# Seven groups of dense expert tiles in two parts of the activation buffer, the next group's U between a group's U and V, four gathered rows moved forward

## The chip, the cores and the metric

The kernel runs on one core of one Trainium2 chip. The metric is the time of one execution on the device, in microseconds (us), the median of several. Everything is float32.

## The reference, cut to what matters

One layer over 512 tokens of width 2048: a mixing part (attention and a recurrence), attention into 256 memory tokens, and an expert part with 16384 experts of one neuron each, eight heads, 16 experts a head and token. The change touches the expert part alone.

```python
def peer_ffn(x, w_pq, sub_keys1, sub_keys2, peer_u, peer_v):
    q = (xt @ w_pq).reshape(T, PEER_HEADS, PEER_QUERY)
    s1, s2 = first half of q . sub_keys1, second half of q . sub_keys2
    v1, i1 = lax.top_k(s1, PEER_TOPK)
    v2, i2 = lax.top_k(s2, PEER_TOPK)
    ...
    top_s, pos = lax.top_k(cand_s, PEER_TOPK)
    idx = jnp.take_along_axis(cand_i, pos, axis=-1)
    gate = jax.nn.softmax(top_s, axis=-1)
    ...
    u_sel = jnp.take(peer_u, ib, axis=0)
    act = jax.nn.gelu(jnp.einsum('thkd,td->thk', u_sel, xb), approximate=False) * gb
    v_sel = jnp.take(peer_v, ib, axis=0)
    return jnp.einsum('thk,thkd->td', act, v_sel)
x = layer_norm(DN_ALPHA * x + y_ffn, ln3_g[l], ln3_b[l])
```

(The line of s1, s2 is shortened; `xb`, `ib`, `gb` are a block's tokens, expert numbers and gates.)

## The kernel before

**Two ways for two halves of the tokens.** The 512 tokens are four blocks of 128. For blocks 0 and 1 the kernel gathers the chosen experts: 128 choices a token and block, so 256 *rows*. A row r is one load of `peer_u` and one of `peer_v` (128 partitions x 8 KB, 1 MB each, an indirect DMA on GpSimd's queue, lines 611 and 622), a dot product on VectorE (line 1739), a Gelu of four rows at a time on ScalarE (`gelu_rows`, line 1318) and an addition into the block's sum on VectorE (line 1750). The dot of row r+4 stands just ahead of the addition of row r. U loads have two buffers, V loads two; a third of each comes in early in the stream. For blocks 2 and 3 (256 tokens) TensorE multiplies with all 16384 experts, in 128 *tiles* of 128: a U tile is 16 matmuls 128x256 (line 1050), ScalarE puts the Gelu of two tiles into the buffer G (`gelu_dense`, line 1333), VectorE multiplies eight tiles at a time with their gates (`weigh(q)`, line 1800), and V quads (4 tiles by 512 output columns, 8 matmuls 128x512, line 1077) sum them in PSUM. In the trace a matmul counts as two records.

**Groups, positions, chunks.** The tiles are cut into groups g of 40, 32, 32 and 24 (`TILES`). G holds one group. TensorE's order is U0, V0, U1, V1, U2, V2, U3, V3, where Ug are a group's U tiles and Vg its V quads: for each of four column chunks c, TILES[g]/4 quads. Each U tile and each V quad takes 1 MB of weights (line 458, SyncE's queue, a ring of four slots). From V0 on they are numbered: a *position* is one U tile or one V quad, 216 in all. V0 is 0 to 39, U1 40 to 71, V1 72 to 103, U2 104 to 135, V2 136 to 167, U3 168 to 191, V3 192 to 215.

**What TensorE waits for in the stream.** A V quad of chunk 0 waits for the product of its eight tiles (`g_ready`). The first quad of a chunk waits until the sum of the chunk two earlier has left its banks (`x_added`, `add_dense`, line 1809 in V0, line 1811 later). A U tile waits for the Gelu of the tiles eight earlier (`gl_done`). Each of these stands in an engine's own list behind other work.

**What stands in VectorE's and ScalarE's lists.** Rows are spread over the positions by `half_pos`: rows 2k and 2k+1 are *due* at a position, and VectorE's program runs through the positions in order, with the products (at `weigh_pos`), the rows due, two last expert choices (at 2 and 3 by number, positions 8 and 15) and, after a chunk's last position, its sum. It doesn't wait for TensorE to reach a position; it can run behind it. `HALVES_BEFORE` (34) says that 68 rows stand ahead of V0. ScalarE's list has the same positions. The rows ahead of V0 are placed by hand (`some_rows(n)`, and `d_route(n, between)`, which puts `between` rows between the two halves of an expert choice). GpSimd issues the row loads in order and, among them, the gates of eight tiles (`load_gates`, from tile 40 on), at places that `GATES_AFTER` works out.

```python
def half_pos(k):
    return 3 + (k - HALVES_BEFORE) * (POSITIONS - 6) // (2 * RSTEPS - HALVES_BEFORE)
...
                if c == 0 and l % 2 == 0:
                    pe.wait_ge(g_ready, FIRST[g] // 8 + l // 2 + 1)
...
                    elif l == 0:
                        pe.wait_ge(x_added, 2 * (g * 4 + c - 2) + tb + 1)
```

**The end.** Block 0's norm (`norm`, line 1488 and on) stands after U3, block 1's within V3 ahead of the last chunk's sum, blocks 2 and 3 are normed after it and written out.

## Time and profile before

| | us |
|---|---|
| median of 3 runs | 3290.2 |
| range of the runs | 3282.97 to 3298.95 |
| the profiled execution | 3295.16 |
| its span, first to last instruction | 3293.5 |
| mean granted TensorE clock over the span | 0.982 |
| TensorE busy with matmuls | 3119.8 (95%) |
| VectorE busy | 2073.9 (63%) |
| moved by DMA | 1029.69 MB, mean 313 GB/s |

Times in the rows count from the span's start. A row of a timeline gives start, duration, engine, line, operation, what it writes and reads, how many were merged (x) and in square brackets the idle time ahead of it and what ended it. Matmul ends are modelled: a merged stretch of 640 records that takes 276 us is TensorE going at one pace. A wait on several semaphores is put down to the one that came last.

### The profile page before, as it was taken

To read this page: it belongs to the slowest core of one execution; us is meant where nothing else is said; L and a number is where in the kernel's file an instruction comes from. 1 tells how busy PE (TensorE), PEld (TensorE's weight loads), DVE (VectorE), ACT (ScalarE), POOL (GpSimd) and SP (SyncE) were. 2 spreads that over 40 slices of the span, in tenths; PEclk is the share of its full clock that TensorE was granted. 3 is DMA by queue.
4 is the path that set the end of the run, shared out by engine and by line. 5 is a ranking of instruction groups with operands and counts; after the bars stand their busy time and mean duration, and the time that the engine had idled before them with its cause. 6 is when DMAs were issued, how large, how long until landed. Compare 5 with 4: busy or idle time off the path is not lost.

```text
span 3293.5 us, 27033 instructions
## 1 busy us (share of the span) xinstructions
PE 3119.8 (95%) x10342; PEld 1889.4 (57%) x10342; DVE 2073.9 (63%) x2874; ACT 367.9 (11%) x653; POOL 682.0 (21%) x557
## 2 busy tenths in 40 slices
PE   8999998899999898999989999999999999999797
PEld 5444443334445577678874447884458853478443
DVE  5356532342668779889997766656566666656675
ACT  1233212320101211112210000000000000000000
POOL 0000000000021134322222333222222333223240
PEclk9999999999999999999999999999999999999899
DMA  6222221047797678998998999999999999999985
GB/s 267 77 77 70 86 65 44 10 166 261 294 408 309 258 316 358 417 387 305 350 350 350 389 422 421 421 415 417 421 421 421 419 419 416 422 421 421 412 368 233
DMA packets 152515, 1029.69 MB, mean 313 GB/s; under 512 B 16464, under 2 KB 21712, under 8 KB 35664
## 3 DMA queue, kind: packets, MB, share of 16 engines
q0 software_dynamic: 78512, 557.88, 41.6%
q1 hardware_dynamic: 73888, 470.24, 36.4%
q8 instruction: 76, 1.25, 0.2%
q14 instruction: 39, 0.32, 0.0%
HBM read 1007.08 MB, written 20.97 MB: 312 GB/s over the span
## 4 chain that ended last, share of the span: by engine, by line
DMA 41%; PE 33%; DVE 18%; issue 4%; ACT 2%; POOL 2%; DVEq 0%; SPq 0%; ACTq 0%; POOLq 0%
DMA arena<-peer_v,arena 40%; PE ps L693 10%; DVE arena L1750 7%; PE ps L1077 4%; PE ps L845 3%; DVE arena L1788 2%; DVE arena L1739 2%; PE ps L935 2%; PE ps L863 2%; PE ps L770 1%; PE ps L1050 1%; PE ps L799 1%; ACT arena L1117 1%; POOL arena L611 1%; PE ps L785 1%
## 5 line engine op out<-in xcount | busy, mean ns | idle before, releaser
L1077 PE MATMUL ps<-arena 128*128 128x512 f32 x2048 | 884.8, 595 | 52.8 <-DVE arena L1800 52.0
L1050 PE MATMUL ps<-arena 128*128 128x256 f32 x4096 | 898.3, 381 | 9.6 <-ACT arena L1333 8.9
L1050 PEld LDWEIGHTS ps<-arena 128*128 128x128 f32 x4096 | 778.7, 191 | 118.9 <-ACT arena L1333 9.7
L1750 DVE SCALAR_TENSOR_TENSOR arena<-arena 128x2048 f32<-128x2048 f32 x256 | 601.8, 2351 | 298.8 <-DMA arena<-peer_v,arena 233.1
L1739 DVE CUSTOM_DVE_ANT_0 arena<-arena 128x2048 f32<-128x2048 f32 x256 | 586.2, 2290 | 288.4 <-DMA arena<-peer_u,arena 286.8
L1077 PEld LDWEIGHTS ps<-arena 128*128 128x128 f32 x2048 | 390.6, 191 | 544.8 <-issue 490.6
L611 POOL DMA_INDIRECT arena<-peer_u,arena x256 | 346.8, 1354 | 1108.3 <-DVE arena L1739 909.3
L622 POOL DMA_INDIRECT arena<-peer_v,arena x256 | 309.2, 1208 | 755.0 <-DVE arena L1750 725.8
L693 PE MATMUL ps<-arena 128*128 128x512 f32 x800 | 345.2, 592 | 1.1 <-ACT arena L1117 1.1
L693 PEld LDWEIGHTS ps<-arena 128*128 128x128 f32 x800 | 151.9, 190 | 192.2 <-issue 192.2
L1117 ACT ACTIVATE arena<-ps 128x512 f32<-128x512 f32 (+3 forms) x247 | 145.2, 611 | 774.9 <-PE ps L855 138.8
L845 PE MATMUL ps<-arena 128*128 128x512 f32 x512 | 220.8, 592 | 0.9 <-ACT arena L1117 0.9
L1318 ACT ACTIVATE arena<-arena 128x4 f32<-128x4 f32 x64 | 13.1, 205 | 1545.1 <-DVE arena L1739 1545.0
L845 PEld LDWEIGHTS ps<-arena 128*128 128x128 f32 x512 | 97.0, 190 | 122.3 <-issue 120.5
L863 PE MATMUL ps<-arena 128*128 128x512 f32 x320 | 139.3, 593 | 2.5 <-ACT arena L1117 2.5
L935 PE MATMUL ps<-arena 128*128 128x256 f32 x640 | 139.2, 379 | 1.7 <-ACT arena L1117 1.7
L935 PEld LDWEIGHTS ps<-arena 128*128 128x128 f32 x640 | 121.3, 190 | 18.9 <-ACT arena L1117 2.2
L863 PEld LDWEIGHTS ps<-arena 128*128 128x128 f32 x320 | 60.6, 190 | 76.2 <-issue 72.5
L1788 DVE TENSOR_TENSOR arena<-arena 128x1024 f32<-128x1024 f32 x64 | 78.1, 1220 | 11.4 <-ACT arena L1117 10.5
L1062 PE MATMUL ps<-arena 128*128 128x128 f32 x512 | 70.0, 281 | 13.3 <-DVE arena L1790 13.2
L1062 PEld LDWEIGHTS ps<-arena 128*128 128x128 f32 x512 | 64.4, 191 | 20.4 <-DVE arena L1790 18.8
L1557 DVE TENSOR_TENSOR arena<-arena 128x512 f32<-128x512 f32 x16 | 11.0, 688 | 99.9 <-ACT arena L1169 99.9
(179 smaller groups left out, 1804.9 us busy)
## 6 DMA issues: line engine op xcount, KB each, us to landing
arena<-peer_ut SPq DMA_DIRECT2D x128, 1024.0 KB
arena<-peer_vt SPq DMA_DIRECT2D x128, 1024.0 KB
arena<-w_row SPq DMA_DIRECT2D x52, 1024.0 KB
arena<-w_mix SPq DMA_DIRECT2D x48, 1024.0 KB
arena<-w_once SPq DMA_DIRECT2D x74, 512.0 KB, 3.5
arena<-w_feat SPq DMA_DIRECT2D x20, 1024.0 KB
dense_gates<-arena SPq DMA_DIRECT2D x8, 2048.0 KB, 7.3
arena<-dense_gates POOLq DMA_DIRECT2D x11, 1024.0 KB, 24.2
```

The lines of the kernel that those rows point to most:

```text
L611: pool.indirect_dma_start(UB[e], None, peer_u, bass.IndirectOffsetOnAxis(ap=IDX[:, r:r + 1], axis=0)).then_inc(u_full[e], 16)
L622: pool.indirect_dma_start(VB[e], None, peer_v, bass.IndirectOffsetOnAxis(ap=IDX[:, r:r + 1], axis=0)).then_inc(v_full[e], 16)
L693: last = pe.matmul(out_ap, tile(t + half)[:, k * P:(k + 1) * P], A[:, kt * S:(kt + 1) * S], start=(kt == 0), stop=(kt == KT - 1))
L845: last = pe.matmul(bank(k), Y[:, b * D + kt * P:b * D + (kt + 1) * P], w[:, i * 512:(i + 1) * 512], start=(kt == NL), stop=(kt == NL - 1))
L863: last = pe.matmul(bank(k), XT[:, kt * P:(kt + 1) * P], w[:, i * 512:(i + 1) * 512], start=(kt == 0), stop=(kt == KT - 1))
L935: last = pe.matmul(ps[:, k + f // 2, (f % 2) * DT:(f % 2 + 1) * DT], w[:, kt * P:(kt + 1) * P], XTD[:, kt * DT:(kt + 1) * DT], start=(kt = ...
L1050: last = pe.matmul(ps[:, (e // 2) % 4, (e % 2) * DT:(e % 2 + 1) * DT], w[:, kt * P:(kt + 1) * P], XTD[:, kt * DT:(kt + 1) * DT], start=(kt ...
L1077: last = pe.matmul(bank(4 + (c % 2) * 2 + tb), G[:, t * DT + tb * P:t * DT + (tb + 1) * P], w[:, i * 512:(i + 1) * 512], start=(t == 0), s ...
L1117: return act.activation(dst, src, ACT.Copy)
L1739: dve.tensor_tensor_reduce(UB[e], UB[e], xrow(b), 1.0, 0.0, ALU.mult, ALU.add, DOT[r // 4 % 2][:, r % 4:r % 4 + 1]).then_inc(u_free, 1)
L1750: dve.scalar_tensor_tensor(out=acc, in0=VB[e], scalar=AV[r // 4 % 2][:, r % 4:r % 4 + 1], in1=acc, op0=ALU.mult, op1=ALU.add).then_inc(v_f ...
L1788: link(dve.tensor_tensor(oh, IOTA.unsqueeze(1).unsqueeze(1).broadcast_to([P, 2, 4, NK]), turn[:, 0:2, here].unsqueeze(3).broadcast_to([P, ...
```

## The change

The tiles are cut into seven groups of 24, 16, 24, 16, 24, 16 and 8. G is 40 tiles long as before, in two parts: groups 0, 2, 4, 6 at slots 0 to 23, groups 1, 3, 5 at slots 24 to 39 (`slot_of`). The head (`HEAD`, 40 tiles) is the U of groups 0 and 1; then the order is V0, U2, V1, U3, V2, U4, V3, U5, V4, U6, V5, V6. Positions: V0 0 to 23, U2 24 to 47, V1 48 to 63, U3 64 to 79, V2 80 to 103, U4 104 to 127, V3 128 to 143, U5 144 to 159, V4 160 to 183, U6 184 to 191, V5 192 to 207, V6 208 to 215. The product of eight tiles stands 13, 21 or 29 positions after the start of its U group; those of the head at positions 0, 1, 2, 10 and 20. `HALVES_BEFORE` is 36: four more rows ahead of V0, two between the sums of d.wo and two in `d_route(4)`, with their Gelu moved ahead of `d_pq(0)` on ScalarE. The other rows are due up to position 202 (before 210). Block 0's norm and block 1's now stand after the last row, in V6; the gain and bias that they need take the gates' two buffers and are loaded on GpSimd's queue, not SyncE's.

```diff
-TILES = [40, 32, 32, 24]
-FIRST = [sum(TILES[:g]) for g in range(4)]
-GCAP = max(TILES)
+TILES = [24, 16, 24, 16, 24, 16, 8]
+NG = len(TILES)
+FIRST = [sum(TILES[:g]) for g in range(NG)]
+HEAD = TILES[0] + TILES[1]
+GCAP = HEAD
+STREAM = [(kind, g) for k in range(NG) for kind, g in (("V", k), ("U", k + 2)) if g < NG]
...
+def slot_of(e):
+
+    g = group_of(e)
+    return e - FIRST[g] + TILES[0] * (g % 2)
...
-HALVES_BEFORE = 34
+HALVES_BEFORE = 36
...
-    return 3 + (k - HALVES_BEFORE) * (POSITIONS - 6) // (2 * RSTEPS - HALVES_BEFORE)
+    return 3 + (k - HALVES_BEFORE) * (POSITIONS - 14) // (2 * RSTEPS - HALVES_BEFORE)
...
-    if q < TILES[0] // 8:
-        return (0, 1, 2, 3, 5)[q]
...
+    if q < HEAD // 8:
+        return (0, 1, 2, 10, 20)[q]
+    g = group_of(8 * q)
+    start = sum(TILES[h] for _, h in STREAM[:STREAM.index(("U", g))])
+    return start + 8 * q - FIRST[g] + 13
...
+            def load_gain3(k):
+                pool.wait_ge(g_ready, NK // 8 - 1 + k)
+                pool.dma_start((GAIN3_G, GAIN3_B)[k], gains[6 + k:7 + k, :].partition_broadcast(P)).then_inc(gain3_in, 16)
...
-                if p == TILES[0] + 6:
+                if p == HEAD + 14:
                     load_gates(4)
...
             exps("b1.max", PR, 6, 0, "b1.exp")
+            gelu_rows()
             d_pq(0)
...
                 if c == 1:
-                    some_rows(2)
+                    some_rows(4)
...
-            d_route(4, 2)
+            d_route(4, 4)
...
+                if g == NG - 1:
+                    rows_until(POSITIONS)
+                    dve.wait_ge(gain3_in, 32)
+                    dve.wait_ge(v_free, HK)
+                    norm(ACC, ACC, GAIN3_G, GAIN3_B, dve_tick).then_inc(y_ready, 1)
                 for c in QUAD:
...
-                    if g == 3 and c == 3:
-                        rows_until(POSITIONS)
+                    if g == NG - 1 and c == 2:
                         dve.wait_ge(v_free, 2 * HK)
                         norm(ACC1, ACC1, GAIN3_G, GAIN3_B, dve_tick).then_inc(y_ready, 1)
                     add_dense(g, c)
```

TensorE, from the last head tiles on: first before, then changed. Lines 1050 and 1074 are the U matmuls (16 a tile), 1077 and 1102 those of V (8 a quad).

```order
L1050 MATMUL ps<-arena 128x256 x88
L1077 MATMUL ps<-arena 128x512 x320
L1050 MATMUL ps<-arena 128x256 x512
L1077 MATMUL ps<-arena 128x512 x256
L1050 MATMUL ps<-arena 128x256 x512
L1077 MATMUL ps<-arena 128x512 x256
L1050 MATMUL ps<-arena 128x256 x384
L1077 MATMUL ps<-arena 128x512 x192
```

```order
L1074 MATMUL ps<-arena 128x256 x88
L1102 MATMUL ps<-arena 128x512 x192
L1074 MATMUL ps<-arena 128x256 x384
L1102 MATMUL ps<-arena 128x512 x128
L1074 MATMUL ps<-arena 128x256 x256
L1102 MATMUL ps<-arena 128x512 x192
L1074 MATMUL ps<-arena 128x256 x384
L1102 MATMUL ps<-arena 128x512 x128
L1074 MATMUL ps<-arena 128x256 x256
L1102 MATMUL ps<-arena 128x512 x192
L1074 MATMUL ps<-arena 128x256 x128
L1102 MATMUL ps<-arena 128x512 x192
```

A group's V now follows the U of the group after it; the last 192 are V5 (128) and V6 (64).

VectorE, at the sums of d.wo (lines 1649 and 1671) ahead of blocks 2 and 3's second norm: first before, then changed. Lines 1739 and 1761 are dots, 1750 and 1772 additions of a row.

```order
L1649 SCALAR_TENSOR_TENSOR arena<-arena,ps 128x512 x2
L1762 TENSOR_TENSOR arena<-arena 128x4
L1739 ISA arena<-arena 128x2048
L1739 ISA arena 128x1
L1750 SCALAR_TENSOR_TENSOR arena<-arena 128x2048
L1739 ISA arena<-arena 128x2048
L1739 ISA arena 128x1
L1750 SCALAR_TENSOR_TENSOR arena<-arena 128x2048
L1649 SCALAR_TENSOR_TENSOR arena<-arena,ps 128x512 x4
L1488 BN_STATS arena<-arena 128x6 x4
```

```order
L1772 SCALAR_TENSOR_TENSOR arena<-arena 128x2048
L1761 ISA arena<-arena 128x2048
L1761 ISA arena 128x1
L1772 SCALAR_TENSOR_TENSOR arena<-arena 128x2048
L1761 ISA arena<-arena 128x2048
L1761 ISA arena 128x1
L1772 SCALAR_TENSOR_TENSOR arena<-arena 128x2048
L1671 SCALAR_TENSOR_TENSOR arena<-arena,ps 128x512 x4
L1510 BN_STATS arena<-arena 128x6 x4
```

Two more rows (the last of the four are shown) stand ahead of the last four sums of d.wo and the norm that follows them.

## Rows read from the trace of the kernel before

**Rows 1.** The page's 40 slices of the span: granted clock, then DMA rate.
```profile
PEclk9999999999999999999999999999999999999899
GB/s 267 77 77 70 86 65 44 10 166 261 294 408 309 258 316 358 417 387 305 350 350 350 389 422 421 421 415 417 421 421 421 419 419 416 422 421 421 412 368 233
```

**Rows 2.** TensorE's timeline from V0's start on (columns as said above).
```profile
1725.39 276.35 PE L1077 MATMUL ps<-arena 128*128 128x512 f32 x640 [9.52 <-DVE arena L1800]
...
2388.39 55.17 PE L1077 MATMUL ps<-arena 128*128 128x512 f32 x128 [0.84 <-DVE arena L1811]
...
2557.77 112.42 PE L1050 MATMUL ps<-arena 128*128 128x256 f32 x512 [3.70 <-ACT arena L1333]
2670.02 41.36 PE L1077 MATMUL ps<-arena 128*128 128x512 f32 x96
2725.32 180.31 PE L1077 MATMUL ps<-arena 128*128 128x512 f32 x416 [13.93 <-DVE arena L1800]
...
2979.90 99.16 PE L1050 MATMUL ps<-arena 128*128 128x256 f32 x448 [5.21 <-ACT arena L1333]
3078.89 27.63 PE L1077 MATMUL ps<-arena 128*128 128x512 f32 x64
3135.04 139.04 PE L1077 MATMUL ps<-arena 128*128 128x512 f32 x320 [28.52 <-DVE arena L1800]
```

**Rows 3.** Stretches: busy us (x) by engine, PEclk, DMA share, GB/s; last, line 1750 alone.
```profile
2711.40:2725.30 13.90, 0.00 (x0) 0.00 (x0) 9.25 (x7) 0.69 (x2) 5.18 (x5) 0.62 1.01 420
3106.50:3135.00 28.50, 0.02 (x1) 0.00 (x0) 23.66 (x32) 0.00 (x0) 7.91 (x5) 0.57 0.86 352
1725.00:1900.00 175.00, 174.61 (x404) 77.40 (x405) 125.93 (x201) 6.41 (x10) 54.16 (x36) 0.99 0.92 367
...
1900.00:2711.00 811.00, 235.17 (x100) 1.00 1.01 420
```

**Rows 4.** VectorE's timeline: the product of tiles 24 to 31.
```profile
1742.06 2.29 DVE L1800 TENSOR_TENSOR arena<-arena 128x2048 f32<-128x2048 f32 x1 [8.93 <-DMA arena<-dense_gates]
```

**Rows 5.** VectorE's timeline: sums after positions 39 and 87, the product of position 136.
```profile
2025.25 1.28 DVE L1809 SCALAR_TENSOR_TENSOR arena<-arena,ps 128x512 f32<-128x512 f32 x2
...
2387.56 1.28 DVE L1811 TENSOR_TENSOR arena<-arena,ps 128x512 f32<-128x512 f32 x2
...
2722.97 2.28 DVE L1800 TENSOR_TENSOR arena<-arena 128x2048 f32<-128x2048 f32 x1
```

**Rows 6.** VectorE's timeline: the two norms (the last row ends at the second) and the end.
```profile
3122.26 2.47 DVE L1488 BATCH_NORM_STATS2 arena<-arena 128x6 f32<-128x512 f32 x4
...
3245.47 2.47 DVE L1488 BATCH_NORM_STATS2 arena<-arena 128x6 f32<-128x512 f32 x4
...
3253.65 2.35 DVE L1494 SCALAR_TENSOR_TENSOR arena<-arena 128x2048 f32<-128x2048 f32 x1
3274.12 1.29 DVE L1811 TENSOR_TENSOR arena<-arena,ps 128x512 f32<-128x512 f32 x2 [18.12 <-PE ps L1077]
```

**Rows 7.** Ahead of V0, VectorE's and TensorE's timelines, in order of time.
```profile
1105.79 2.28 DVE L1739 CUSTOM_DVE_ANT_0 arena<-arena 128x2048 f32<-128x2048 f32 x1
...
1114.74 2.47 DVE L1649 SCALAR_TENSOR_TENSOR arena<-arena,ps 128x512 f32<-128x512 f32 x4
...
1138.15 1.97 PE L855 MATMUL ps<-arena 128*128 128x128 f32 x16 [2.06 <-DVE arena L1494]
...
1174.20 0.16 DVE L1762 TENSOR_TENSOR arena<-arena 128x4 f32<-128x4 f32 x1 [17.38 <-ACT arena L1318]
...
1257.78 3.40 PE L985 MATMUL ps<-arena 128*128 128x128 f32 x16 [5.84 <-ACT arena L1117]
```

**Rows 8.** VectorE's timeline: additions of two rows in a run of four.
```profile
954.00 2.35 DVE L1750 SCALAR_TENSOR_TENSOR arena<-arena 128x2048 f32<-128x2048 f32 x1 [1.80 <-issue]
...
962.03 2.35 DVE L1750 SCALAR_TENSOR_TENSOR arena<-arena 128x2048 f32<-128x2048 f32 x1 [2.37 <-DMA arena<-peer_v,arena]
```

**Rows 9.** The page's DMA issues: out<-in, queue, kind, count, KB each.
```profile
arena<-peer_vt SPq DMA_DIRECT2D x128, 1024.0 KB
```

More of the change, by code:

```diff
@@ L84, with group_of @@
 SLOTS = 4
-TILES = [40, 32, 32, 24]
-FIRST = [sum(TILES[:g]) for g in range(4)]
-GCAP = max(TILES)
+TILES = [24, 16, 24, 16, 24, 16, 8]
[4 more added lines that the diff above has]
+STREAM = [(kind, g) for k in range(NG) for kind, g in (("V", k), ("U", k + 2)) if g < NG]
+def group_of(e):
+    return max(g for g in range(NG) if FIRST[g] <= e)
+def slot_of(e):
+    g = group_of(e)
+    return e - FIRST[g] + TILES[0] * (g % 2)
 PQ_AFTER = [2, 5, 8, 11]
@@ L631, in _ @@
                     v_row(4 * j + s)
-                    for q in range(5, NK // 8):
+                    for q in range(5, NK // 8 + 2):
                         if GATES_AFTER[q] == 4 * j + s:
-                            load_gates(q)
+                            if q < NK // 8:
+                                load_gates(q)
+                            else:
+                                load_gain3(q - NK // 8)
         @block.tensor
@@ L1076, in v_quad @@
                         t = 4 * l + i
-                        last = pe.matmul(bank(4 + (c % 2) * 2 + tb), G[:, t * DT + tb * P:t * DT + (tb + 1) * P],
+                        at_g = slot_of(FIRST[g] + t) * DT + tb * P
+                        last = pe.matmul(bank(4 + (c % 2) * 2 + tb), G[:, at_g:at_g + P],
                                          w[:, i * 512:(i + 1) * 512], start=(t == 0), stop=(t == TILES[g] - 1))
                 used(last, f"V{g}.{c}.{l}")
-            for t in range(TILES[0]):
+            for t in range(HEAD):
                 if ONEHOT_FROM <= t < ONEHOT_FROM + DT // 16:
@@ L1101, in _ @@
                     last.then_inc(tb_mm, 1)
-            for g in range(4):
-                for c in QUAD:
-                    for l in range(TILES[g] // ET):
-                        v_quad(g, c, l)
-                if g < 3:
-                    for t in range(TILES[g + 1]):
-                        u_tile(g + 1, t)
+            for kind, g in STREAM:
+                if kind == "U":
+                    for t in range(TILES[g]):
+                        u_tile(FIRST[g] + t)
+                else:
+                    for c in QUAD:
+                        for l in range(TILES[g] // ET):
+                            v_quad(g, c, l)
             assert order == PE_STEPS and at[0] == W_AT[W_UNITS[-1]]
@@ L1439, in _ @@
             gelu_rows()
-            for t in range(t, TILES[0], 2):
-                gelu_dense(0, t)
-                if t == TILES[0] - 6:
+            for t in range(t, HEAD, 2):
+                gelu_dense(t)
+                if t == HEAD - 6:
                     gate_exps(12)
@@ L1454, in _ @@
             p = 0
-            for g in range(4):
-                for _ in range(TILES[g]):
+            for kind, g in STREAM:
+                for t in range(TILES[g]):
+                    if kind == "U" and t % 2:
+                        gelu_dense(FIRST[g] + t - 1)
                     rows_until(p)
                     p += 1
-                if g < 3:
-                    for t in range(TILES[g + 1]):
-                        if t % 2:
-                            gelu_dense(g + 1, t - 1)
-                        rows_until(p)
-                        p += 1
             rows_until(POSITIONS)
@@ L1942, in _ @@
                     add_dense(g, c)
-                    if g == 3:
+                    if g == NG - 1:
                         last = last_stats(c)
-                if g < 3:
-                    for t in range(TILES[g + 1]):
-                        for i in range(TILES[g + 1] // 8):
-                            if weigh_pos(FIRST[g + 1] // 8 + i) == p:
-                                weigh(FIRST[g + 1] // 8 + i, i)
-                        rows_until(p)
-                        p += 1
-                    if g == 2:
-                        dve.wait_ge(gain3_in, 32)
-                        dve.wait_ge(v_free, HK)
-                        norm(ACC, ACC, GAIN3_G, GAIN3_B, dve_tick).then_inc(y_ready, 1)
-                if g == 3:
-                    link(last)
+            link(last)
             for tb in range(DB):
```

112 lines of the change are left out of this document (57 added, 55 removed).

## The prediction

> **What bounds the kernel now.** I read the slices of the page first, then TensorE's timeline from 1725 us with what ended each of its waits, and last, in the same stretch, VectorE's timeline and what DMA moved. In the slices the clock row is nearly all nines, and from 1894 to 3128 us the core moves 412 to 422 GB/s [rows 1]: two resources are full at once, TensorE and DMA. In the stream that the change rearranges, TensorE runs 40 positions in 276.35 us, 6.91 us each, and stands still five times: 0.84, 3.70, 13.93, 5.21 and 28.52 us, 52.2 us in all [rows 2]. The two long ones are waits for the gates' product (line 1800), 52.0 us with the 9.52 ahead of V0; the 3.70 and 5.21 are Gelus (line 1333), the 0.84 a sum (line 1811) [rows 2]. 216 positions at 6.91 us are 1492 us; V0's start to the last matmul's end is 3274.1 - 1725.4 = 1548.7 us [rows 2]. So 52.2 us are stalls and 4.6 us slower matmuls around them (the granted clock is 0.62 and 0.57 over the two long stalls, between the levels of 1.2 and 2.4 GHz [rows 3]). Those 56.8 us are all that any order of this stream could win on TensorE.
>
> Why is the product late? V2 starts at 2670.0 and V3 at 3078.9 [rows 2], but the products due then (positions 136 and 192) run at 2723.0 and 3132.7 (the end of the second stall) [rows 2, 5]: **VectorE is 53 us, nearly eight positions, behind its own list.** It does not wait for TensorE; it waits for row loads. From 1900 to 2711 us it adds 100 rows [rows 3] while six gate loads go through the same queue: 206 loads in 811 us, 3.94 us each, at 420 GB/s in total [rows 3]. A row is two loads, 7.87 us.
>
> **The lag, as a sum.** Before, 2 rows are due every 2.234 positions, 0.895 a position: VectorE needs 0.895 x 7.87 = 7.04 us for a position that TensorE does in 6.91, so the lag grows 0.14 us a position and 3.9 us with each gate load. Test: the rows due by position 38 end at 2025.3, with TensorE at 38 at 1725.4 + 38 x 6.91 = 1988, a lag of 37; the sum of chunk 1 of V1 (rows due by 87) comes at 2387.56 against 2326, a lag of 61 [rows 2, 5]. The rule gives 37 + 49 x 0.14 + 4 x 3.9 = 60. It holds.
>
> **Part 1: the products leave the path: -56.8 us.** In the new order eight tiles' product is placed 13 positions or more after the start of their U group, and their V group begins 27 positions or more after that (11 for V6). At a lag of 60 us the margin of 27 x 6.91 = 187 us isn't touched. The 42.4 us of long stalls go; the 9.8 us of short ones and the 4.6 us of slow clock I take off here too and count again in part 3.
>
> The matmuls, 10342 of them, the products and the sums of the rest are as before in number, but for 24 more sums (56 for 32) of 0.64 us each on VectorE [rows 5], which has idle time beside every row, and TensorE takes a U or a V position in the same 6.91 us (16 of U, the slow clock after a stall among them, take 112.42 [rows 2]): the new order itself costs nothing.
>
> **Part 2: four rows earlier: +11 us ahead of V0.** Two of them stand between the sums of d.wo. There VectorE is on the path: its sums for d.wo 2 and 3 start at 1114.74, as soon as two rows are done, the norms follow, and TensorE waits 2.06 us for the second one at 1138.15 [rows 7]. Two rows cost at least 2 x 4.47 us (1105.79 to 1114.74 for two, dot and add [rows 7]) and up to 8 us each where both buffers are empty (954.00 to 962.03 [rows 8]): 9 to 16, here about 10, since the first two find their data there. After b1's probabilities VectorE sits 17.38 us until the Gelu at 1174 [rows 7]; the change puts that Gelu earlier, four rows fit in the gap, and it takes up the first delay. But in d_route(4) four rows stand where two stood, with buffers just drained: 9 to 16 us again, and this chain is what TensorE waits for at 1257.78 (5.84 us) [rows 7]. So both engines come 8 to 15 us late to tile U0, and no wait for anything else hides it. I take 11, near the lower end, since the data of at least two rows is there.
>
> **Part 3: what is late next: +44 us.** A V group's chunk c writes into the banks of chunk c-2, so TensorE waits at chunk 2 for the sum of chunk 0, and that sum stands in VectorE's list behind all rows due by then. With 40 and 32 tiles a chunk is 10 or 8 positions and VectorE may be 9 positions (62 us) late; at a lag of 61 the stall was 0.84 us [rows 2]. With 16 tiles a chunk is 4 positions: the last rows ahead of the sum are due 5 positions before it is needed in V1 and 6 in V3 and V5, less 2 us for the sum: 33 and 39 us. With 24 tiles it is 7 or 8, 46 and 53 us. The lag is above that.
> The new lag: two rows are due every 202/92 = 2.196 positions, 0.911 a position; 0.911 x 7.87 - 6.91 = 0.26 us of growth a position. The product of tiles 24 to 31 no longer stands ahead of the first rows; it waited 8.93 us for its gates and took 2.28 [rows 4], so the rows start 11 us sooner. At position 38 the lag is 37 - 11 + 35 x 0.126 = 30. From there to 202, where the last rows are due, it would grow by 164 x 0.26 = 43 us and by 10 loads of gates and gain, 39 us: 112 us if TensorE never stood. It can't: V5 lets it pass with 39 at most, some 37 at position 202. The 75 us between are taken off by stalls. In a stall all of DMA goes to the rows: 420 GB/s in the 13.9 us stall [rows 3], against 2 x 1.0486 MB in 7.87 us, 267 GB/s. So a microsecond of stall takes off 1.57, and the stalls come to 75 / 1.57 = **48 us**, most of it at chunk 2 of V3 (about 20), the rest in V1, V4, V5 and U4.
> The other bound is bytes. Before, the last row ends at 3245.4, 1520 us after V0's start [rows 6]. Now 8 row loads are gone and, with TensorE at position 207, some 4.5 weight loads aren't due yet: 12.5 loads of 1024 KB [rows 9] at 421 GB/s [rows 1], 2.49 us each, 31 us. VectorE's first norm, 10.5 us long, starts at 3122.26 between two rows, in a stall whose stretch moved only 352 GB/s [rows 3, 6]; it now comes after the last row: 10 us. The earlier start puts 11 us of rows, 2.9 MB, into a stretch that averaged only 367 GB/s [rows 3]: 6 us. The last row would end 1473 us after V0's start, which at position 202 (1395 us) and a lag of 37 leaves **41 us** of stalls. I take 44, between the two, and 4 us of slow clock (before 4.6 for 52.2).
>
> The page "DMA: Bandwidth & Descriptors" of the Trainium skill (Where 436 GB/s comes from) says that for HBM to SBUF the HBM side, about 358 GB/s, binds. The trace disagrees: 420 GB/s and more over most of 1200 us [rows 1, 3]. By the page's figure a load would cost 2.93 us, the 12.5 loads 37 us and the second bound 35 us of stalls; the trace decides.
>
> **The end** stays: the last group of 8 tiles needs the last row's end + 13 us (a norm of 10.5, 3245.47 to 3256.00 [rows 6], and a sum) by position 212; at 207.5 + 2 positions there are 17 us to spare. The second norm has the two positions of chunk 2, 13.8 us for 10.5. The gain's second half is now the last load of GpSimd's queue, behind the last row; it lands about one load, 4 us, later, within the 17. From the last matmul's end to the end of the span 19.4 us stay [rows 6].
>
> **Sum.** -56.8 + 11 + 44 + 4 = +2 us: 3295.2 us of the profiled execution become 3297; it lies 5 us above the median of the three runs, 3290.2, which becomes **3292**.
>
> **Rivals.** *A, faster: the narrow groups don't hold TensorE.* If only V6 binds (last row + 13 us at position 212) the stalls are 1473 + 13 - 1464 = 22 us and the sum is -56.8 + 11 + 22 + 2 = -22: 3268. With the delay of part 2 absorbed as well, 3258. For it: the lag thresholds rest on one stall of 0.84 us. Against: list and banks are plain in the code, and the 3.70 and 5.21 us stalls show that a lag of 60 us bites elsewhere too. *B, slower: a stall doesn't speed the rows.* If rows alone don't use the freed DMA time, the stalls are 75 us at factor 1: +31 us, 3323; it turns to slower by 0.5% from a factor under about 1.3 (59 us of stalls). For it: over the long stall only 352 GB/s moved. Against: that stretch holds the norm; the other one moved 420 [rows 3]. [...] *C, the head costs more:* 16 us twice with no gap to take it up, +32 - 11: 3313, slower. *D, the change doesn't do what it says:* products still late. It would take a lag of 187 us; under 1%.
>
> **How the numbers follow.** Forecast (stalls 38 to 52, head 8 to 15): 56%, 3283 to 3304. A 22%, B 10%, C 9%, the rest no case named here. 16.5 us (0.5%) is about what a measurement can tell from no change. The forecast's range lies within it. Faster 0.24, same 0.56, slower 0.20. The range reaches to A's and C's times: 3266 to 3314.
>
> **What would show it.** In the trace after: no wait of V's matmul for the product except ahead of V0; V0 starting near 1736; waits of the V line on the sum's line, largest in V3 and V5, 30 to 45 us in all; DMA at 420 in them; the last row about 1473 us after V0's start. Wrong if the waits for sums are under 25 us or over 60, or V0 starts before 1730 or after 1745.

## The result, and the profile after

Of the kernel before, 7 runs have a median of 3288.98 us, of the changed kernel, 7 runs, 3308.26 us (3300.25 to 3320.02). The ratio is 1.0058, with a 95% interval of 1.004 to 1.0076: **slower by 0.6%**, where I had forecast 3292 and no change; 3308 lies within the range. The profiled execution of after is the fastest of its seven (3300.25 us, span 3298.6), that of before lies 6 us above the median of its seven: the two profiles are 5 us apart where the medians are 19.

TensorE's timeline of after from V0's start on (start, length, engine, line, operation, count, in brackets the idle time ahead and what ended it). Line 1102 is V's matmul, 1074 U's, 1823 the product, 1834 the sum of the groups after V0, 1772 the addition of a row:

```profile
1735.24 106.13 PE L1102 MATMUL ps<-arena 128*128 128x512 f32 x240 [9.38 <-DVE arena L1823]
1845.24 64.55 PE L1102 MATMUL ps<-arena 128*128 128x512 f32 x144 [3.87 <-DMA arena<-peer_vt]
1909.63 165.92 PE L1074 MATMUL ps<-arena 128*128 128x256 f32 x768
2075.39 82.68 PE L1102 MATMUL ps<-arena 128*128 128x512 f32 x192
2166.17 30.16 PE L1102 MATMUL ps<-arena 128*128 128x512 f32 x64 [8.10 <-DVE arena L1834]
...
2637.24 55.10 PE L1102 MATMUL ps<-arena 128*128 128x512 f32 x128
2708.99 57.58 PE L1102 MATMUL ps<-arena 128*128 128x512 f32 x128 [16.66 <-DVE arena L1834]
...
2965.66 84.72 PE L1102 MATMUL ps<-arena 128*128 128x512 f32 x192 [6.18 <-DVE arena L1834]
...
3167.46 111.98 PE L1102 MATMUL ps<-arena 128*128 128x512 f32 x256 [6.89 <-DVE arena L1834]
```

Against [rows 2] the two waits for the product, 13.93 and 28.52 us, are gone and so are the Gelus'; in their place stand four waits for a sum, 37.8 us, and one of 3.87 for a V load. Five stalls are 41.7 us, where five were 52.2. From V0's start to the start of the last matmul it was 1548.1 us, now it is 1543.6 (to that matmul's end, as the prediction counts, 1548.7 and 1544.2).

The view of stretches, over three of the sum waits, and line 1772 alone over the stretch of [rows 3] (busy us by engine, then granted clock, DMA share, GB/s), then VectorE's timeline at the longest wait:

```profile
2158.00:2166.20 8.20, 0.10 (x2) 0.06 (x1) 5.42 (x5) 0.00 (x0) 3.04 (x4) 0.68 1.01 423
2692.30:2709.00 16.70, 0.04 (x2) 0.04 (x1) 12.48 (x10) 0.00 (x0) 6.72 (x4) 0.63 1.01 408
...
3160.50:3167.50 7.00, 0.11 (x2) 0.07 (x1) 5.44 (x5) 0.20 (x1) 0.94 (x1) 0.78 1.02 424
...
1900.00:2711.00 811.00, 236.00 (x101) 0.98 1.01 419
```

```profile
2700.97 2.35 DVE L1772 SCALAR_TENSOR_TENSOR arena<-arena 128x2048 f32<-128x2048 f32 x1 [2.77 <-issue]
...
2705.90 2.35 DVE L1772 SCALAR_TENSOR_TENSOR arena<-arena 128x2048 f32<-128x2048 f32 x1 [0.23 <-DMA arena<-peer_v,arena]
2708.17 1.28 DVE L1834 TENSOR_TENSOR arena<-arena,ps 128x512 f32<-128x512 f32 x2
```

TensorE stands, its clock is granted at 0.63 to 0.78 of the full one, DMA still moves 408 to 424 GB/s, and VectorE takes rows as they land; the sum that TensorE needs comes right behind the last row listed ahead of it.

Ahead of V0, in order of time, to compare with [rows 7] (VectorE's rows, d.wo's sums, then TensorE's waits):

```profile
1103.87 2.35 DVE L1772 SCALAR_TENSOR_TENSOR arena<-arena 128x2048 f32<-128x2048 f32 x1 [1.40 <-DMA arena<-peer_v,arena]
...
1112.31 2.35 DVE L1772 SCALAR_TENSOR_TENSOR arena<-arena 128x2048 f32<-128x2048 f32 x1 [2.10 <-DMA arena<-peer_v,arena]
1114.58 2.48 DVE L1671 SCALAR_TENSOR_TENSOR arena<-arena,ps 128x512 f32<-128x512 f32 x4
...
1127.55 3.68 PE L880 MATMUL ps<-arena 128*128 128x128 f32 x16 [8.76 <-DVE arena L1516]
1137.99 3.68 PE L880 MATMUL ps<-arena 128*128 128x128 f32 x16 [6.76 <-DVE arena L1516]
...
1268.42 3.79 PE L1010 MATMUL ps<-arena 128*128 128x128 f32 x16 [13.96 <-ACT arena L1143]
```

TensorE now waits 15.5 us for the two norms (before 2.06) and 13.96 for the dense keys (before 5.84). In the profile of after everything stands 12 us earlier by then: its first row is added at 910.67 us, in before at 922.52. So V0's start, 1735 against 1725, hides part of what the head lost.

**A ruler.** From the first row's addition to V0's start it is 802.9 us in before, and 802.1, 802.3, 802.3 and 809.6 in the four runs below that leave the four rows where they were; with the four rows moved it is 824.6 in after and 827.7 to 834.9 in six others. The means are 803.8 and 830.5. The runs' tables below give, in us: *stream*, V0's start to the start of the last matmul; *stalls*, TensorE's idle time in it; *last row*, from V0's start to the end of the last addition of a row; *tail*, the start of the last matmul to the end of the span. Each from the profile of one execution; ratios are to the kernel before, with 95% intervals.

| kernel | ratio | stream | stalls | last row | tail |
|---|---|---|---|---|---|
| before | | 1548.1 | 52.2 | 1520 | 20.0 |
| after | 1.0058 [1.004, 1.0076] | 1543.6 | 41.7 | 1474 | 19.8 |

### The profile page after: what moved, and what is told of

It is laid out like the page before. It is cut to its first block, busy times and chain, and to the rows that moved or that the text cites. A ratio compares the mean times of both kernels' runs of the same rounds, so it can differ in the third digit from the quotient of the medians.

```text
span 3298.6 us, 27067 instructions
## 1 busy us (share of the span) xinstructions
PE 3117.6 (95%) x10342; PEld 1888.6 (57%) x10342; DVE 2089.0 (63%) x2898; ACT 370.1 (11%) x653; POOL 682.7 (21%) x559
## 3 DMA queue, kind: packets, MB, share of 16 engines
q0 software_dynamic: 78800, 559.97, 41.7%
## 4 chain that ended last, share of the span: by engine, by line
DMA 40%; PE 33%; DVE 19%; issue 4%; POOL 2%; ACT 2%; DVEq 0%; ACTq 0%; SPq 0%; POOLq 0%
DMA arena<-peer_v,arena 40%; PE ps L718 10%; DVE arena L1772 7%; PE ps L1102 5%; PE ps L870 3%; DVE arena L1810 2%; DVE arena L1761 2%; PE ps L960 2%; PE ps L888 2%; PE ps L795 1%; PE ps L1074 1%; ACT arena L1143 1%; DVE arena L1699 1%; PE ps L810 1%; POOL arena L633 1%
## 5 line engine op out<-in xcount | busy, mean ns | idle before, releaser
L1102 PE MATMUL ps<-arena 128*128 128x512 f32 x2048 | 895.5, 600 | 51.1 <-DVE arena L1834 37.8
L633 POOL DMA_INDIRECT arena<-peer_u,arena x256 | 336.9, 1316 | 1084.5 <-DVE arena L1761 882.8
L644 POOL DMA_INDIRECT arena<-peer_v,arena x256 | 318.6, 1244 | 755.2 <-DVE arena L1772 736.6
L960 PEld LDWEIGHTS ps<-arena 128*128 128x128 f32 x640 | 123.2, 193 | 19.7 <-ACT arena L1143 2.2
L1086 PE MATMUL ps<-arena 128*128 128x128 f32 x512 | 70.0, 281 | 13.2 <-DVE arena L1812 13.1
L1086 PEld LDWEIGHTS ps<-arena 128*128 128x128 f32 x512 | 64.4, 191 | 20.4 <-DVE arena L1812 18.7
```

Of the source, the lines that this page charges most:

```text
L633: pool.indirect_dma_start(UB[e], None, peer_u, bass.IndirectOffsetOnAxis(ap=IDX[:, r:r + 1], axis=0)).then_inc(u_full[e], 16)
L644: pool.indirect_dma_start(VB[e], None, peer_v, bass.IndirectOffsetOnAxis(ap=IDX[:, r:r + 1], axis=0)).then_inc(v_full[e], 16)
L960: last = pe.matmul(ps[:, k + f // 2, (f % 2) * DT:(f % 2 + 1) * DT], w[:, kt * P:(kt + 1) * P], XTD[:, kt * DT:(kt + 1) * DT], start=(kt = ...
L1102: last = pe.matmul(bank(4 + (c % 2) * 2 + tb), G[:, at_g:at_g + P], w[:, i * 512:(i + 1) * 512], start=(t == 0), stop=(t == TILES[g] - 1))
```

## Experiments

**My theory:** the new order gains little in the stream, four rows ahead of V0 cost what they give back, and the sums wait since rows that the transfers bring late are listed ahead of them. Rivals: another cause of the sums' waits; a cheap head; a loss in the order alone.

### The order alone, the rows alone, and after once more

The rows alone are the kernel before with these lines changed; the order alone is the changed kernel with the same lines changed back:

```diff
-HALVES_BEFORE = 34
+HALVES_BEFORE = 36
+            gelu_rows()
-                    some_rows(2)
+                    some_rows(4)
-            d_route(4, 2)
+            d_route(4, 4)
```

> The change without its four moved rows: the new order of groups, 68 rows ahead of V0, 188 rows due by position 202. Theory (the end is set by how fast DMA brings rows and weights, and the stalls in V are where VectorE's lag is taken off): V0 starts near 1725 us as before the change (1735 with the rows moved), eight row loads more lie in the stream, 2.49 us each, so the waits for sums grow from 38 us to 55 to 62 us and the last row ends some 1496 us after V0's start (1476 changed). The run is about 10 us slower than the changed kernel, ratio to before 1.007 to 1.011. Rival (the ten microseconds at the head are what made the change slow, and the order costs nothing): 10 us faster than the changed kernel, ratio to before 1.000 to 1.003.

> The kernel before with the four rows moved ahead of V0 and nothing else. Theory: V0 starts 10 us later; the stream has eight loads less and its lag grows 0.15 us a position less, so the five stalls shrink from 52 us to about 32; ratio to before 0.995 to 0.999. Rival (rows at the head cost their 10 us and give nothing back, since VectorE's lag is not what delays the products): ratio 1.002 to 1.004.

> The changed kernel once more, for a second profile beside the others of this series. The profile at hand is its fastest run (3300 us; the median of seven is 3308). Expected: ratio 1.004 to 1.008, four waits for sums, 38 to 48 us in all, and the difference between a 3300 and a 3310 run in the stalls of the stream, not ahead of V0.

| kernel | ratio | stream | stalls | last row | tail |
|---|---|---|---|---|---|
| order alone | 1.0055 [1.0041, 1.007] | 1569.7 | 67.1 | 1494 | 19.7 |
| rows alone | 1.0008 [0.9993, 1.0023] | 1526.5 | 30.4 | 1499 | 20.0 |
| after again | 1.0062 [1.0048, 1.0075] | 1544.2 | 44.4 | 1472 | 19.7 |

**The loss comes without the four rows.** The rest of the change alone costs 0.55%, and its stream is 21.6 us longer than before. This kernel holds more than the new groups, though: its rows are due by position 202 instead of 210, and the norms and a gates' load have moved too. No run takes these apart, but the paced kernel without the four rows, below, has the same groups with the rows due later, and is no slower than before. So the groups by themselves need not lose; most likely they do together with rows listed this early. TensorE's timeline of the order alone:

```profile
2719.67 56.62 PE L1102 MATMUL ps<-arena 128*128 128x512 f32 x128 [29.58 <-DVE arena L1833]
...
3177.69 112.94 PE L1102 MATMUL ps<-arena 128*128 128x512 f32 x256 [15.90 <-DVE arena L1833]
```

The wait at V3's chunk 2 is as long as the longest product wait that the order removes. The four rows shorten the stream by 21.6 us in the old order and by 26.1 in the new one (1569.7 to 1543.6), yet the ratio moves by +0.0008 and +0.0003: so the head costs 24 us (21.6 + 0.0008 x 3290) and 27 (26.1 + 1), to within some 5 and 8 us by the ratios' intervals; the ruler says 26.7. My expectations had each wrong by this one number: I gave the rows alone 0.995 to 0.999 (measured 1.0008) and the order alone 1.007 to 1.011 (measured 1.0055), though the stalls came as told, 30.4 us for 32 and 58.5 us of sum waits for 55 to 62. TensorE's waits for the norms and the dense keys in the head of the rows-alone kernel (1090 to 1300 us; engine, line, for whom, us, times, longest) are 36.1 us, against 12.1 in the same stretch of before:

```profile
PE ps L855 <- DVE arena L1495: 17.4, 2, 10.7
PE ps L985 <- ACT arena L1117: 13.7, 2, 12.6
PE ps L985 <- DVE arena L1650: 5.0, 1, 5.0
```

After once more repeats the stream within 1 us. I had expected the spread between runs to be in the stream; between these two profiled executions it is ahead of V0 (1735.2 and 1744.2).

### Which pair costs the head

Each takes the kernel before and moves two of the four rows. The edit below is that of the pair at d.wo; the other has `d_route(4, 4)` in place of `some_rows(4)`. Both also put the Gelu ahead of `d_pq(0)`, as the change does, and since 35 halves need one Gelu of rows fewer ahead of V0 than 36, ScalarE's last one before the stream is left out.

```diff
-HALVES_BEFORE = 34
+HALVES_BEFORE = 35
...
+            gelu_rows()
             d_pq(0)
...
-            gelu_rows()
             for t in range(t, TILES[0], 2):
...
-                    some_rows(2)
+                    some_rows(4)
```

> The kernel before with one pair of rows moved alone: two more rows behind the second d.wo addition, so 35 halves instead of 34 stand ahead of the stream. Theory (the moved rows find their buffers empty: 7 to 9 us a row instead of 4.6, and TensorE then waits for the norms of the dense streams): the waits for those norms grow from 2 us to 12 to 16 us, the activation products start 10 to 14 us later than in the kernel before (1720 to 1725 us there), the stream from there to the last product is 10 to 12 us shorter than 1548; ratio 0.999 to 1.002. Rival (the head's loss comes from the fourth routing, not from here): norm waits stay below 6 us, the products start within 5 us of before, ratio 0.996 to 0.998.

> The kernel before with the other pair alone: four rows instead of two in the fourth routing. Theory: the norm waits stay at 2 us, the wait of the dense key transposes grows from 5.8 us to 11 to 14 us, the products start 7 to 10 us later than before, the stream is 10 to 12 us shorter; ratio 0.998 to 1.001. Rival (this pair is free, it lies beside other work): products start within 3 us of before, ratio 0.996 to 0.998.

| kernel | ratio | stream | stalls | first row to V0 |
|---|---|---|---|---|
| pair at d.wo | 1.0078 [1.0053, 1.0103] | 1540.0 | 44.1 | 845.7 |
| pair at the route | 1.0069 [1.0043, 1.0094] | 1539.8 | 43.6 | 838.9 |

The pair at d.wo, then the pair at the route, TensorE's waits from 1090 to 1300 us:

```profile
PE ps L855 <- DVE arena L1494: 17.1, 2, 10.3
PE ps L985 <- ACT arena L1117: 8.7, 3, 6.4
```

```profile
PE ps L889 <- ACT arena L1117: 14.9, 1, 14.9
PE ps L985 <- ACT arena L1117: 7.4, 4, 3.8
PE ps L855 <- DVE arena L1494: 2.0, 1, 2.0
```

The pair at d.wo makes TensorE wait 15 us more for the norms (17.1 for 2.1), a little over the 12 to 16 us expected. Under the other pair it is not the rows that TensorE waits for. ScalarE's timeline of that kernel shows what stands ahead of the wait at line 889:

```profile
1179.39 0.21 ACT L1318 ACTIVATE arena<-arena 128x4 f32<-128x4 f32 x1 [14.83 <-DVE arena L1739]
1179.50 1.01 ACT L1117 ACTIVATE arena<-ps 128x1024 f32<-128x1024 f32 x1
```

The eviction that TensorE needs (line 1117) stands behind a Gelu of rows (line 1318) that waits 14.83 us for its dots: with the Gelu ahead of `d_pq(0)`, every later one stands one place earlier in ScalarE's list, and here the rows that it takes are not yet done. In before, with fewer rows ahead, TensorE waits 1.3 us at this line. So the 14.9 us come with the second edit. The same holds for what comes after. U0's start to V0's start is 449 us in both kernels and 426 to 432 in every other one here; from 1290 to 1760 us ScalarE's Gelus of rows wait 131.3 us for dots in both, in nine waits, and 24.1 us, in one, in before and in the rows-alone kernel. I had expected ratios of 0.999 to 1.002 and 0.998 to 1.001; the measured 1.0078 and 1.0069 carry this edit and say nothing of the pairs.

The stretch ahead of it does: from the first row's addition to U0's start it is 370 to 378 us in the five kernels without the move (mean 374), 396.5 with the pair at d.wo, and 397 to 407 in the seven with all four rows (mean 402). **The pair at d.wo costs about 22 of the 28 us**, the pair at the route some 6, to within about 5 us, since each kernel has one profile. A kernel with the Gelu moved and no rows was not run.

### Sums earlier in VectorE's list

```diff
             def position(p):
+                if p in sums:
+                    add_dense(*sums[p])
...
-                    add_dense(g, c)
+                    if g in (0, NG - 1):
+                        add_dense(g, c)
```

(`sums` holds the sums of V1 to V5, each four positions earlier than its own.)

> The changed kernel with the sums of V1 to V5 four positions earlier in VectorE's list, so that they no longer stand behind rows due in the last four positions. Theory: TensorE's 38 us of waits for these sums go, but the rows' loads still need their bytes: the last row ends 5 to 15 us later than 1476 us after V0's start, and the last group's chunk 2 waits for it. Gain against the changed kernel 12 to 22 us, ratio to before 0.999 to 1.003. Rival 1 (only the place of the sums made the change slow): the whole 38 us and some 8 us of slow clock behind the stalls go, ratio 0.992 or less. Rival 2 (the waits move to Gelus, products or weights within the stream): no gain, ratio 1.005 or more.

Measured: ratio 1.0049 [1.0032, 1.0066]; stream 1536.9, stalls 37.3. TensorE's waits in the stream:

```profile
PE ps L1075 <- ACT arena L1359: 20.4, 2, 13.5
PE ps L1103 <- DVE arena L1835: 13.2, 1, 13.2
```

The sums' waits fall from 37.8 to 13.2 us, and 20.4 us of waits for Gelus appear: ScalarE has the dense Gelus behind those of rows, and they wait for the same late rows. Only 7 us of the stream are gained, and the ratio can't be told from the changed kernel's (1.0062 beside it); I had expected 0.999 to 1.003. It came nearer the second rival, that the waits move. With a lag as large as this one, moving one kind of work ahead of the rows brings up the next.

### Is it the transfers?

Two kernels take bytes from V's weight loads and leave every list as it is. In both, half of each V tile's weights isn't loaded, so they compute something else.

```diff
+                if unit[0] == "V":
+                    sp.dma_start(W2[s][0:64, :], src[0:64, :]).then_inc(wb_full[s], 16)
```

> The changed kernel with the weight loads of the V tiles cut to the upper 64 of 128 partitions: every V load carries half its bytes, and half of each V tile's weights is left as it was, so the output is another. Nothing else in any list moves. Theory (rows are late since the transfers move 417 to 422 GB/s and no more, so a sum listed behind rows waits for bytes): with about 54 MB fewer between the first product and the last row the rows keep up with their places, the sum waits fall from 38 us to under 8 us, products' start to last product 1500 to 1512 us; the rate drops below 400 GB/s. Rival (the sums wait for VectorE's own work or for how the row loads are issued): sum waits stay above 25 us, the stream above 1530 us.

```diff
+                if unit[0] == "V":
+                    sp.dma_start(W2[s][:, 0:PW // 2], src[:, 0:PW // 2]).then_inc(wb_full[s], 16)
```

> The changed kernel with the V weight loads cut to half their columns on all 128 partitions: packets of 4096 bytes (181 ns each in the changed kernel's trace) in place of 8192 bytes (314 ns), so each of the V loads gives the 16 DMA engines about 1.1 us back; half of each V tile's weights is left as it was, so the output is another. (With the upper 64 partitions alone the packets of 8192 bytes took 413 to 512 ns instead of 314 and the rows came later, not earlier.) Theory (sums wait since the rows ahead of them in VectorE's list are late by what the transfers can carry): with 110 us of transfer time less, the rows keep up with their places, sum waits fall from 38 us to under 8 us, products' start to last product 1500 to 1515 us. Rival (the sums wait for VectorE's own work or for how row loads are issued): sum waits stay above 25 us and the stream above 1530 us.

| kernel | ratio | stream | stalls | last row | tail |
|---|---|---|---|---|---|
| upper 64 partitions | one run, 3393.3 us | 1617.2 | 111.3 | 1557 | 19.7 |
| half the columns | 0.9908 [0.9879, 0.9936] | 1491.4 | 1.7 | 1397 | 19.7 |

The same stretch, within V1, of the one and of the other:

```profile
2100.00:2150.00 50.00, 49.45 (x116) 21.59 (x114) 27.09 (x19) 1.38 (x4) 15.02 (x12) 1.00 1.01 301
```

```profile
2100.00:2150.00 50.00, 50.00 (x118) 22.23 (x117) 38.65 (x29) 0.41 (x2) 18.04 (x17) 1.00 1.02 415
```

The first is a miss that taught something: I had expected the sum waits to fall under 8 us, and they rose to 103. DMA's share stays full at 301 GB/s, a packet of 8192 bytes takes 413 ns (rows) and 512 ns (weights) on average there, against 314 and 316 in after; half the partitions did not give half the time. The second is the clean test: all sum waits vanish, one stall of 1.70 us for a V load stays, and the stream is shorter even than the 1500 to 1515 us expected. In after, the rows due at position 125 are added 62 us after TensorE's arrival there; here 17. **The sums wait for rows and the rows for transfers: shown.** It also gives a floor for the stream: 1491.4 - 1.7 = 1489.7 us.

### Rows listed at the rate of the transfers

If lateness ahead of a sum is the harm, the rows can be listed later. Between V0's start and the last row, two rows take about 16 us, 2.3 positions of 6.91; the changed kernel lists them 2.20 apart. The last group is relaxed too, and the gates' load (line 513) goes back to where it was.

```diff
-    return 3 + (k - HALVES_BEFORE) * (POSITIONS - 14) // (2 * RSTEPS - HALVES_BEFORE)
+    return 3 + (k - HALVES_BEFORE) * (POSITIONS - 2) // (2 * RSTEPS - HALVES_BEFORE)
-                if p == HEAD + 14:
+                if p == HEAD + 6:
...
                 if g == NG - 1:
-                    rows_until(POSITIONS)
...
-                    if g == NG - 1 and c == 2:
+                    if g == NG - 1 and c == 3:
+                        rows_until(POSITIONS)
```

> The changed kernel with the rows listed at the rate at which the transfers bring them: the halves stand 2.33 positions apart instead of 2.20, so that weighings and sums of a group are no longer listed behind rows that have not arrived; in the last group the sums of its first chunks stand ahead of the last rows, the first norm ahead of that group, and the gates' load goes back to where a full ring hides it. Theory (the sum waits of 38 us are rows that stand ahead of the sum in VectorE's list while the transfers, at 420 GB/s, are behind): the rows still arrive at the same times, the last 1470 to 1485 us after the first product, TensorE's stalls in the stream fall from 42 to under 15 us, products' start to last product 1505 to 1520 us; ratio to before 0.989 to 0.996 (with a head as in the changed kernel). Rival 1 (the sums wait for something that does not depend on the list): stalls stay above 30 us, ratio 1.003 or more. Rival 2 (rows listed later are also fetched later, and the transfers fall below 415 GB/s): last row over 1490 us after the first product, ratio 0.998 to 1.004.

The same with the four rows where they were:

> The same pacing, without the four rows moved: 34 halves ahead, halves 2.28 positions apart. Theory: the products start 15 to 25 us earlier than in the paced kernel, the last row arrives 1495 to 1508 us after their start, so rows are 20 to 30 us behind their places at the end and the last group waits for them: stalls 15 to 30 us, ratio within 0.003 of the paced kernel's. Rival (the four rows are worth more in the stream than at the head once the sums are free of the rows): ratio 0.004 or more above the paced kernel's; or the reverse, 0.004 or more below it.

With, besides, early sums and `min(3 + (k - HALVES_BEFORE) * 7 // 3, POSITIONS - 2)`:

> The paced kernel without the four rows, rows 2.33 positions a half apart also with 34 halves ahead (held at two positions before the end), and the sums of groups V1 to V5 listed four positions earlier. Theory (the transfers set when rows arrive, the list alone decides who waits behind them; the head costs 24 us with the four rows and gives back 21): products start at 1720 to 1725 us, stalls 10 to 20 us, last row 1505 to 1525 us after the products' start, stream 1510 to 1525 us, ratio 0.990 to 0.995. Rival 1 (four more rows in the stream are too many: the last rows arrive after TensorE is done, the tail takes what the stalls gave): tail over 35 us, ratio 0.996 to 0.999. Rival 2 (earlier sums only move the wait to ScalarE's gelu, as in the kernel with early sums): stalls of 25 us or more, ratio 0.996 to 0.998.

And this last line alone, in the kernel before:

> The kernel before in its own order of groups, with only the places of the rows changed: 2.33 positions a half instead of 2.23. Theory A (most of the loss is rows listed too early, in any order of groups): the five stalls of 52 us fall to 25 to 35 us, ratio 0.992 to 0.996. Theory B (in this order a product waits for the last gelu and weighing of its own group whatever the rows do, 9 us in each of the later groups, and rows listed later meet the last group): stalls 38 to 50 us, ratio 0.997 to 1.001, and then the narrow interleaved groups are what makes pacing pay.

| kernel | ratio | stream | stalls | last row | tail |
|---|---|---|---|---|---|
| paced | 0.9985 [0.9972, 0.9998] | 1513.1 | 20.3 | 1508 | 24.9 |
| paced, no rows moved | 0.9974 [0.9961, 0.9986] | 1534.1 | 38.9 | 1529 | 24.5 |
| the same, early sums | 0.9988 [0.9971, 1.0005] | 1518.0 | 25.6 | 1535 | 46.5 |
| before, paced | 0.9972 [0.9957, 0.9987] | 1505.9 | 11.8 | 1528 | 51.7 |

The mechanism came as told, the gain only in part. The paced kernel's stream is 30.5 us shorter than after's (I said 1505 to 1520), its stalls 20.3 (I said under 15), its tail 5 us longer, its ratio 0.007 lower; my range of 0.989 to 0.996 was a wrong sum, since 25 us from 1.0058 give 0.998. And the last row comes 34 us later than in after, as rival 2 had it, though the transfers kept 418 to 422 GB/s in every slice of the page from 1900 to 3190 us: a row listed later is fetched later. Pacing the kernel before does as much by itself. TensorE's only stalls in its stream, and VectorE's end:

```profile
3063.88 16.84 PE L1077 MATMUL ps<-arena 128*128 128x512 f32 x32 [4.76 <-DVE arena L1800]
3087.72 140.46 PE L1077 MATMUL ps<-arena 128*128 128x512 f32 x320 [7.01 <-DVE arena L1800]
```

```profile
3247.07 2.35 DVE L1750 SCALAR_TENSOR_TENSOR arena<-arena 128x2048 f32<-128x2048 f32 x1 [0.27 <-DMA arena<-peer_v,arena]
...
3259.90 1.28 DVE L1811 TENSOR_TENSOR arena<-arena,ps 128x512 f32<-128x512 f32 x2
```

TensorE is done at 3228.2, the last row at 3249.4, and block 1's norm, the last sum and the norms of blocks 2 and 3 take 30 us more. The stalls fell by 40 us, the tail grew by 32. Early sums do the same to the other kernel. **This fits one budget, the transfers,** where the lists only choose where it is paid: by TensorE in the middle, or behind it at the end. Paced before and paced new order without the rows (3281.0 and 3285.1 us) are both faster than before by a quarter of a per cent; I can't tell them apart. The four rows again: paced with them, less without them, is +0.0011, 4 us, while the stream is 21 us shorter: 24 to 25 us for the head, a third time (to within some 8 us).

The other three expectations missed as well. Paced without the rows I had given 15 to 30 us of stalls and the last row by 1508 us; they are 38.9 and 1529, though the ratio lies within the 0.003 told. With early sums I had given 0.990 to 0.995; what came is the first rival, the tail taking what the stalls gave. For the paced kernel before neither theory holds: the stalls fell to 11.8 us, further than either had it, and the ratio of 0.9972 is that of the theory that saw little gain.

## Why the prediction was right or wrong

- **Two resources full, rows late by the transfers: right**, shown by the loads of half the columns.
- **Part 1, products off the path: right.** The product is waited for only ahead of V0, 9.38 us. But the 4.6 us of slow clock didn't leave: with the floor of 1489.7 us, before has 1548.1 - 52.2 - 1489.7 = 6.2 us besides its stalls, after 12.2. I had taken 4 for after. By three kernels it goes by the number of stalls more than by their length: 12.9 us for the 8 of the order alone (67 us), 16 for the 7 of the upper-64 kernel (111 us), 3.1 for two in the paced one (20 us).
- **Part 3, 44 us of new waits: right in kind and size.** 37.8 us, largest in V3 (16.66), the last row 1474 us after V0's start for 1473. In the stalls DMA moved 408 to 424 GB/s, against rival B, and V1, V3, V4 and V5 all held TensorE, against rival A. The page "DMA: Bandwidth & Descriptors" of the Trainium skill (Where 436 GB/s comes from) says that the HBM side, about 358 GB/s, binds from HBM to SBUF; the estimate from that figure was 35 us of stalls. The trace of after disagrees with the figure, as that of before did: it moved 419 GB/s over 811 us.
- **A term that was missing: 3.87 us.** The gates' load for tiles 32 to 39 moved eight weight loads later in SyncE's queue (start, length, line, count; last, the time from issue to landing of the V load behind it):

```profile
1800.21 14.06 SPq L474 DMA_DIRECT2D arena<-peer_vt  x3
1814.31 0.43 SPq L513 DMA_DIRECT2D arena<-dense_gates  x1
1820.81 20.93 SPq L474 DMA_DIRECT2D arena<-peer_vt  x4
```

```profile
DMA to landing us min/median/max: 24.4/24.4/24.4
```

 The next V load leaves at its usual 6.9 us after the one before it, but it lands 24.4 us later, where the five ahead of it took 4.8 to 9.5; the gates' load itself takes 25.9. TensorE is there three positions, 20.6 us, after the issue, at 1841, and waits the 3.87 us that are missing. In the paced kernel, with the load at its old place, the V load behind it lands after 18.8 us and nobody waits. The wait is in all kernels with the load there (3.8 to 4.8 us; 1.7 with half the columns) and in none of the three paced ones in the new order, which have it back; since those differ in the rows as well, that its place alone makes the wait is likely, not shown.
- **Part 2, the head: the step that failed.** I took 11 us from bounds of 9 to 16 for each pair: one pair, at the route, counted, and a gap was to take up the other. Measured are 24 to 27, and the pair that I had let vanish is the one that costs, about 22. At d.wo the third and fourth row took 7.0 and 8.4 us with their buffers empty, where I had said about 10 for both, and TensorE's waits for the norms grew by 13.5 us (15.5 for 2.06); the 17 us gap of [rows 7], which I let take this up, comes behind the norms and so took up nothing. The pair at the route, which I had at 9 to 16, costs some 6: the waits for the dense keys grew by 7 us (line 1010, 16.9 us in all from 1090 to 1300 us; before 10.0). From 170 us after the first row's addition to U0's start TensorE's waits are 17 to 20 us in the five kernels without the move and 40 to 44 in the seven with it, so about 22 of the 27 us are seen as waits and the rest is not traced. Rival C (3313, 9%) came nearest in time, for another reason than its 16 us twice; by the measured head the sum is -4.5 + 24 to 27 = +20 to +23, and 3289 + 20 is 3309.
- **The sum:** -56.8 + 44 + 4 = -8.8 was forecast for the stream, -4.5 measured (stalls down by 10.5, slower matmuls up by 6.0); 11 for the head, 24 to 27 measured. The medians are 19.3 us apart where I said 2: of the 17 us missed, 4 are the stream's and 13 to 16 the head's. That 3308 still lies inside the stated range is owed to its width, which reached to rival C's time. A slip beside it: rival B's terms (75 of stalls, 4 of slow clock) add up to +33 us and 3323, not to the +31 written.
- **"Wrong if V0 starts after 1745":** it started at 1735.24, near the 1736 told, and the step was wrong all the same. The profile was of an execution whose first row came 12 us early. An absolute start was the wrong thing to name; an interval from a mark ahead of the edit (802 to 810 us in the five kernels without it) would have shown it.
- **What I had not asked:** what the rest does without the four rows. With 34 halves ahead the stream is 21.6 us longer; the change as a whole looked neutral in my sum because the rows' credit lay in the same term as this loss.

## What to carry to other kernels

When one resource is full for the whole stage, a reordering only moves the wait: count what the narrow groups' shorter slack lets through (by the prediction's arithmetic a 16-tile group here stands 33 to 39 us of lateness, a 32-tile one about 60), and price the order and each added edit separately. A Gelu, or any step that takes work in fixed portions, moves only with all of its portion: half of it ahead cost some 19 us in two kernels here. Work moved out of a full stage costs its full time where it goes if an engine there is on the path with empty buffers, and idle time further on does not take it up; four rows gave back 21 to 26 us and cost 24 to 27. List late-arriving work at the rate at which it arrives, and then look at the tail.

## What the runs showed of the hardware

- Weight loads onto 64 of 128 partitions took about four fifths of the DMA time of full ones (64 packets of 512 ns against 128 of 316), and the rows' packets beside them grew longer too: packets of 8192 bytes went from 314 to 413 (rows) and 512 ns (weights) on average, the rate in V groups from 417 to 301 GB/s with DMA's share at 1.01. Halving the columns instead halved the weights' share of DMA (37.5% to 18.4% from 2100 to 2150 us): the rows got 342 and 327 GB/s in two stretches of 50 us in V groups, 262 and 270 in the same stretches of after.
- In the thirteen kernels with sum, product or Gelu waits the stream is longer than floor and stalls together by 1.2 to 2.5 us for each stall, with little regard to length (after: five stalls of 4 to 17 us, 12.2 us; before: five of 1 to 29 us, 6.2 us). In the longest stalls the granted clock was 0.57 to 0.63.
- Of two profiled executions of the changed kernel the streams differ by 0.6 us, the starts of V0 by 9. The spread of single runs, 20 us in after, thus seems to lie ahead of the stream; what makes it stays open.
- A load of 1 MB of gates in 1024 packets of 1 KB took 25.9 us to land, and the next 1 MB weight loads on the same queue 19.6 to 24.4 us, against 4.8 to 9.5 just ahead of it.
